# Attention's outputs as fp16 pairs, turned to features inside attention, and an out-projection on them

## What is computed

```python
def trunk_layer(x, xt, ...):
    h = modulate(rms_norm(x, g_attn), sh_a, sc_a)          # and ht for the context tokens
    ... = split_mixer_inputs(h @ w_in, qk_g)               # q, k, v of three head groups
    o = jnp.concatenate([window_attention(...),            # group A, 6 heads
                         neighbourhood_attention(...),     # group B, 4 heads
                         global_block_attention(...)], -1) # group C, 6 heads
    x = x + ga_a * (o @ w_out)
    x = x + ga_f * swiglu(modulate(rms_norm(x, g_ffn), sh_f, sc_f), w_gate, w_up, w_down)
    if update_ctx:                                         # layer 0 only
        ...                                                # the same for xt
```

## Time and profile before

| | before |
|---|---|
| median of 3 runs | 1800.26 us |
| profiled execution, whole | 1800.2 us |
| its span, first to last instruction | 1798.4 us |
| mean granted clock of PE, share of full speed | 0.982 |
| PE busy | 1684.0 us (94%) |
| PE weight loads busy | 1241.0 us (69%) |
| DVE busy | 970.4 us (54%) |
| ACT busy | 662.0 us (37%) |
| POOL busy | 787.5 us (44%) |

### The profile page before, as it was taken

One profiled execution on the slowest core, in us unless ns is written; L12 is line 12 of the kernel. 1 busy time (PEld: TensorE's weight loads), 2 busy tenths in 40 slices (PEclk: granted clock), 3 DMA queues, 4 the chain that ended last, 5 costly groups with the idle time before them and its releaser, 6 DMA issues. The chain is left out here.

```text
span 1798.4 us, 27888 instructions
## 1 busy us (share of the span) xinstructions
PE 1684.0 (94%) x11035; PEld 1241.0 (69%) x11035; DVE 970.4 (54%) x1715; ACT 662.0 (37%) x1218; POOL 787.5 (44%) x575
## 2 busy tenths in 40 slices
PE   7999988977989999999999999997987999999998
PEld 3688877866856678666876687786876645745646
DVE  3544488895458841686428844456995612122112
ACT  3222267775233410233013113225875354053130
POOL 2244435662424563344413343542233657458363
PEclk9999999999989999999999999999999999999999
DMA  9344353322124423245226422443103324334332
GB/s 316 47 107 114 98 139 86 91 59 71 47 71 141 120 82 103 83 131 162 72 70 188 137 62 57 114 101 107 19 2 82 83 71 117 94 90 109 83 82 82
DMA packets 314351, 174.99 MB, mean 97 GB/s; under 512 B 87518, under 2 KB 309614, under 8 KB 314222
## 3 DMA queue, kind: packets, MB, share of 16 engines
q1 hardware_dynamic: 284686, 143.70, 30.3%
q10 hardware_dynamic: 29536, 29.51, 5.1%
HBM read 159.04 MB, written 2.83 MB: 90 GB/s over the span
## 5 line engine op out<-in xcount | busy, mean ns | idle before, releaser
L889 PE MATMUL acc<-act,pair_w 128*128 128x512 f16 x3168 | 582.9, 345 | 7.2 <-ACT act L1283 4.2
L889 PEld LDWEIGHTS acc<-act,pair_w 128*128 128x128 f16 x3168 | 308.8, 99 | 268.2 <-DVE act L1607 10.0
L889 PE MATMUL acc<-act,split_w 128*128 128x512 f32 (+1 forms) x1920 | 381.0, 357 | 8.8 <-DVE act L1871 2.8
L889 PEld LDWEIGHTS acc<-act,split_w 128*128 128x128 f32 x1920 | 308.9, 191 | 62.2 <-DVE act L1871 4.5
L889 PE MATMUL acc<-hidden,split_w 128*128 128x512 f32 (+1 forms) x1584 | 309.2, 357 | 6.6 <-POOL split_w L655 3.6
L652 POOL TENSOR_SCALAR split_w<-raw_w 128x1024 fp32r<-128x1024 f32 (+1 forms) x120 | 126.6, 1055 | 427.6 <-PE acc L889 333.5
L889 PEld LDWEIGHTS acc<-hidden,split_w 128*128 128x128 f32 x1584 | 260.0, 188 | 53.0 <-POOL split_w L655 5.3
L655 POOL TENSOR_TENSOR split_w<-raw_w,split_w 128x1024 fp32r<-128x1024 f32 (+1 forms) x120 | 280.3, 2336 | 10.0
L758 POOL TENSOR_SCALAR pair_raw<-pair_raw,weight_scale 128x1024 f32<-128x1024 f32 x88 | 106.2, 1207 | 357.5 <-ACT pair_w L1457 357.5
L1934 DVE SCALAR_TENSOR_TENSOR mod_acc<-mod_chunk,silu_c,mod_acc 128x256 f32<-128x256 f32 x280 | 223.7, 842 | 4.0
L1632 DVE SCALAR_TENSOR_TENSOR x_t<-acc,mod,x_t 128x512 f32<-128x512 f32 x96 | 60.4, 659 | 257.1 <-PE acc L889 256.6
(11 more groups left out here) (189 smaller groups left out, 1883.3 us busy)
## 6 DMA issues: line engine op xcount, KB each, us to landing
mod_chunk<-in_w_mod ACTq DMA_DIRECT2D x28, 1024.0 KB, 5.2
pair_raw<-in_w_gate SPq DMA_DIRECT2D x44, 512.0 KB, 4.1
pair_raw<-in_w_up SPq DMA_DIRECT2D x44, 512.0 KB, 5.5
raw_w<-in_w_in SPq DMA_DIRECT2D x64, 256.0 KB, 3.7
raw_w<-in_w_down SPq DMA_DIRECT2D x32, 512.0 KB, 4.2
raw_w<-in_w_mod SPq DMA_DIRECT2D x24, 512.0 KB, 4.2
mod_start<-in_w_mod SPq DMA_DIRECT2D x8, 1024.0 KB, 11.7
ks<-q_split SPq DMA_DIRECT2D x64, 96.0 KB, 2.2
```

Of the source, the lines that this page charges most:

```text
L889: mm = pe.matmul(acc[slot][:, a:b], weights[:, part == 2, k, :], moving[:, part == 1, k, a:b], start=(k == 0 and part == 0), stop=(k == n ...
```

## The change

Attention's output is no longer kept as fp32. POOL makes a high and a low fp16 part of each group's output in three passes (`output_high`, `output_whole`, `output_low`) into `o16`. PE turns both parts with fp16 transposes, one feature tile at a time, for latent tokens (part 0) and context tokens (part 1) apart, at steps of attention that the table `OUT_TURNS` fixes; the turned tile goes into one of the three rotating PSUM banks, and one ACT instruction (two for tiles 3 and 4) copies both parts, relatively scaled, into `out16`. Only the turns whose step is past the loop's work come after it.

The out-projection takes fp16 pairs on both sides. Its 8 weight tiles have raw buffers of their own for all 8 (`out_raw`) and four for the pairs (`out_w`). Squares and roundings of tiles 0 to 2 are put into attention's steps on ACT (`OUT_SQUARE_STEP`, `OUT_ROUND_STEP`), one sum and scale into `OUT_SUM_STEP`; those of tiles 3 to 7 stand between ACT's other work during the out-projection. Tiles 3 to 7 are loaded when attention's last output is ready. `residual` takes a gate that has the scales multiplied in. Five small DVE instructions and one small product per layer make the outputs' common scale in the in-projection. The sums of weights, for gate and up also, are one bf16 product of the upper halves of fp32 sums instead of an fp32 one.

```diff
+OUT_ORDER = (0, 1, 2, 5, 6, 7, 3, 4)
+OUT_SUM_STEP = [92, 56]
+OUT_SQUARE_STEP = [(88, 89, 90), (51, 52, 53)]
+OUT_ROUND_STEP = [(94, 95, 96), (58, 59, 61)]
+N_OUT_EARLY = 3
...
+OUT_TURNS = [
+    [(38, 0, 0), (40, 1, 0), (42, 2, 0), (47, 0, 1), (49, 1, 1), (51, 2, 1), (74, 5, 0), (75, 6, 0), (76, 7, 0),
+     (79, 5, 1), (83, 6, 1), (86, 7, 1), (90, 3, 1), (94, 4, 1), (99, 3, 0), (100, 4, 0)],
+    [(26, 0, 0), (29, 1, 0), (37, 2, 0), (50, 5, 0), (53, 6, 0), (60, 7, 0), (66, 3, 0), (68, 4, 0)],
+]
...
+            out += [("o", n) for n, _, _ in turns_at(l, i)]
+            if i == OUT_SUM_STEP[l]:
+                out.append(("w", l))
...
+        out_w = [place(f"out_w{i}", [P, 2, 8, P], F16, split_at_ + (0, 8192, 4096, 12288)[i]) for i in range(4)]
...
-        o = place("o", [P, 6, D], F32)
+        o16 = place("o16", [P, 6, 2, D], F16)
+        out16 = [place(f"out16_{m}", [P, 2, TOK], F16, b0 + where) for m, where in
+                 enumerate((47104, 50176, 53248, 16384, 19456, 56320, 59392, 62464))]
+        out_raw = [raw_w[0], raw_w[1], place("out_raw2", [P, 8, P], F32, b0 + 22528)] + [
+            place(f"out_raw{j}", [P, 8, P], F32, a0 + 4096 * (j - 3)) for j in range(3, KT)]
...
-                    sp.wait_ge(split_ready, ring_of[u] - 1)
+                    if j < 2:
+                        sp.wait_ge(split_ready, ring_of[u] - 1)
+                    elif j < N_OUT_EARLY:
+                        sp.wait_ge(scores, LAYER_STEPS[l][-16] + 1)
+                    else:
+                        sp.wait_ge(o_ready, sum(N_GROUPS[:l + 1]))
...
-                        sp.wait_ge(ot_ps, l * KT + 1)
+                        sp.wait_ge(o_ready, sum(N_GROUPS[:l + 1]))
...
-                    if j in (2, 3):
-                        load_pair(j - 2)
+                    if j in (4, 6):
+                        load_pair(j // 2 - 2)
...
+            def split_out(l, j):
+
+                u = u_out(l) + j
+                pool.wait_ge(out_hi, KT * l + j + 1)
+                pool.tensor_scalar(out_raw[j][:, :, :], out_raw[j][:, :, :], out_scale[:, 1, j:j + 1], 0.0, ALU.mult, ALU.add
+                                   ).then_inc(hi_w, 1)
+                pool.wait_ge(hi_w, ring_of[u] + 1)
+                pool.tensor_tensor(out_w[j % 4][:, 1, :, :], out_raw[j][:, :, :], out_w[j % 4][:, 0, :, :], ALU.subtract
+                                   ).then_inc(split_ready, 1)
...
+                    pool.tensor_tensor(output_piece(k, 0), output_sum(k), inverse_sums(k), ALU.mult).then_inc(o_hi, 1)
+
+                def output_whole(k):
+                    gk = k + sum(N_GROUPS[:l])
+                    pool.wait_ge(o_hi, gk + 1)
+                    pool.tensor_tensor(output_sum(k), output_sum(k), inverse_sums(k), ALU.mult).then_inc(o_mul, 1)
+
+                def output_low(k):
+                    gk = k + sum(N_GROUPS[:l])
+                    pool.wait_ge(o_mul, gk + 1)
+                    pool.tensor_tensor(output_piece(k, 1), output_sum(k), output_piece(k, 0), ALU.subtract).then_inc(o_ready, 1)
...
+                    if k == N_GROUPS[0] - 2:
+                        split_out(l, 0)
+                    output_high(k)
+                    output_whole(k)
+                    output_low(k)
                     if 16 <= k < 20:
                         for i in range(4):
                             bias_tables(k - 16, i)
-                for i in range(4 * N_GROUPS[l] + 8 if l else 0):
+                for i in range(4 * N_GROUPS[l] + 10 if l else 0):
                     if i < 4 * N_GROUPS[l]:
                         minus_top(LAYER_STEPS[l][0] + i)
                     if i == 4 * N_GROUPS[l]:
-                        split_next(0)
+                        split_out(l, 0)
                     if i >= 11 and i % 4 == 3:
-                        take_output((i - 11) // 4)
+                        output_high((i - 11) // 4)
+                    if i >= 12 and i % 4 == 0:
+                        output_whole((i - 12) // 4)
+                    if i >= 13 and i % 4 == 1:
+                        output_low((i - 13) // 4)
...
+                high = weight_sum[:, 2 * f:2 * f + 2].bitcast(BF16)[:, 1:4:2]
+                pe.matmul(mod_ps[:, 0:2], ones16[:, :], high, start=True, stop=True).then_inc(weight_ps, 1)
...
+                def turn_output(n, m, part):
+
+                    free_bank(("o", n))
+                    pe.wait_ge(o_ready, sum(N_GROUPS[:l]) + OUT_GROUPS[l][m, part] + 1)
+                    if n == 0:
+                        pe.wait_ge(masks_ready, 1)
+                    bank = turned_at[BANK_AT["o", n] % 3].bitcast(F16)
+                    for p in range(2):
+                        for t in ((0, 1, 2, 3), (4, 5))[part]:
+                            a = 512 * p + P * (t - 4 * part)
+                            mm = pe.transpose(bank[:, a:a + P], o16[:, t, p, P * m:P * m + P], ident_h[:, :])
+                    mm.then_inc(ot_ps, 1)
...
-                outputs_to_features(0)
...
+                for n, m, part in turns_at(l, g1 + 4 - g0):
+                    turn_output(n, m, part)
...
-                    dense(u % 2, split_w[u % 2], 8, act, width(l), output_tile if j == 0 else last_output if j == KT - 1 else None)
+                    for i, k in enumerate(OUT_ORDER):
+                        if j == 0:
+                            pe.wait_ge(ot_taken, last_turn[k])
+                        if 1 <= j < KT - 2 and i == 1:
+                            sum_out(j + 2)
+                        if j == KT - 1 and i == KT - 1:
+                            sum_first_squares(2 * l + 1, width(l))
+                        for part in (0, 2, 1):
+                            for a, b in parts_of(width(l)):
+                                mm = pe.matmul(acc[u % 2][:, a:b], out_w[j % 4][:, part == 2, k, :], out16[k][:, part == 1, a:b],
+                                               start=(i == 0 and part == 0), stop=(i == KT - 1 and part == 1))
+                    mm.then_inc(unit_done, 1)
...
+                    sc.activation(out_squares[:, :], out_raw[j][:, :, :].rearrange("p k n -> p (k n)"), ACT.Square,
+                                  accum_out=out_sum[:, j:j + 1]).then_inc(out_sq, 1)
...
+                    sc.wait_ge(out_scaled, out_call(l, j))
+                    sc.wait_ge(unit_done, u_out(l) + (j - 3 if j >= 4 else 0))
+                    sc.activation(out_w[j % 4][:, 0, :, :], out_raw[j][:, :, :], ACT.Copy, scale=out_scale[:, 1, j:j + 1]
+                                  ).then_inc(out_hi, 1)
...
+                    if m in (3, 4) and part == 0:
+                        for p in range(2):
+                            i = sc.activation(out16[m][:, p, 0:LAT].rearrange("p (r c) -> p c r", r=ROWS),
+                                              bank[:, 512 * p:512 * p + LAT].rearrange("p (c r) -> p c r", r=ROWS), ACT.Copy, scale=scale)
+                    else:
+                        a, b = ((0, LAT), (LAT, TOK))[part]
+                        i = sc.activation(out16[m][:, :, a:b], bank.rearrange("p (s c) -> p s c", s=2)[:, :, 0:b - a], ACT.Copy, scale=scale)
+                    i.then_inc(ot_taken, 1)
...
+                    if k == 0:
+                        square_out(3)
+                    elif k + 2 < KT:
+                        round_out(k + 2)
+                    if k + 4 < KT:
+                        square_out(k + 4)
...
+                    ve.tensor_scalar(out_gate[:, j, 0:nb], mod[:, l, 2 * KT + j, 0:nb], out_scale[:, 0, j:j + 1], o_back[:, 0:1],
+                                     ALU.mult, ALU.mult).then_inc(out_gated, 1)
+                    ve.wait_ge(out_gated, KT * l + j + 1)
+                    if 1 <= j < KT - 2:
+                        scale_out(j + 2, j + 3, small[:, j + 2:j + 3])
                     ve.wait_ge(unit_done, u_out(l) + j + 1)
-                    residual(j % 2, x_t[:, j, :], l, mod[:, l, 2 * KT + j, :], w)
+                    residual(j % 2, x_t[:, j, :], l, out_gate[:, j, :], w)
```

201 lines of the change are left out of this document (128 added, 73 removed).

## The result

The changed kernel takes 1816.11 us (median of 7 runs, 1808.96 to 1819.86) against 1800.26 us for the kernel before (7 runs, 1796.07 to 1805.84): a ratio of 1.0081, 95% interval 1.0058 to 1.0104. It is slower, by 10 to 19 us. The forecast was 1803, slower by 2.9, with a range up to 1813. The profiled execution took 1816.1 us with a span of 1814.3; the one of before took 1800.2 with 1798.4, so the traces differ by 15.9 us.

A forecast was written before the change was run, and what follows sets the result against it. Attention was taken as held by VectorE with ScalarE close behind, the turn into the out-projection by a chain of small steps. -14.6 + 9 + 0.7 + 10 - 3 + 0.8 = +2.9 on 1800.2 gave 1803 us, range 1788 to 1813.

The forecast's parts named there:

- Layer 0's attention and turn: Layer 0: inserted work costs attention 9 us; the stretch from last weighing through out-projection takes 69.7 against 84.3, gaining 14.6.
- Layer 1's attention: Layer 1's attention: turns, squares, roundings and scale steps inserted between exponential and rounding delay VectorE, costing 10 us.
- The ring of layer 1: Layer 1's out-projection: dependent ScalarE and VectorE laps of 7 to 8 us make TensorE wait 8; stretch 0.7 us longer.
- The sums of weights ... save 3 (bounds 0 and 6): Between dense units: one bf16 product instead of two fp32 ones halves 0.14 us for 44 sums, saving 3 us.
- Norm and down stages of layer 1: Behind layer 1's out-projection: -1.0 us, from shares of the 3 us sums saving and the 0.8 us small costs.
- rival 2: Layer 1's out-projection: TensorE falls to the low clock, units 3 to 7 take 10.36 us each, about 1817; chance 0.12.
- Rival 3: Layer 1's out-projection: loads come later than reckoned and adds block, a stall of 15 us, about 1810; chance 0.11.

The follow-up runs named there:

- experiment 1: Changed kernel with VectorE's last 8 modulation accumulations moved behind the first residual in down stages 1 and 2: 1805.14 us, ratio 1.0025.
- experiment 2: Changed kernel with loads, squares, sums and roundings of weight pairs 0 and 1 moved behind the out-projection's own tiles, both layers: 1809.21 us, ratio 1.0046.
- experiment 9: Changed kernel with GpSimd's split passes of the second next pair behind down tiles 3 and 5 instead of 1 and 2: 1801.71 us, ratio 1.0002.
- experiment 12: Changed kernel with both VectorE's last accumulations and GpSimd's split passes moved later in the down stages: 1800.73 us, ratio 1.0004.
- experiment 3: Kernel before with only the sums of weight squares as one bf16 product instead of two fp32 ones: 1801.51 us, ratio 0.9997.
- the fair pair: Changed kernel and kernel before with bf16 sums, both with later accumulations and later split passes: 1800.73 and 1785.38 us.

## Why the prediction was wrong

The two profiled executions differ by 15.9 us, and the sum had 2.9. Of the 13 between them, 4.6 lie in layer 0's second down stage, 3.1 behind layer 1's norm, 2.0 in layer 1's turn, and 1.6 each in layer 0's turn and layer 1's attention.

- **Layer 0's attention and turn**: right. +9.4 for 9, and 70.1 us for 69.7. The last output was ready 3.1 us after the last weighing (3.0 forecast). To the norm the gain is 13.1 instead of 14.6, mostly because the last weighing itself now starts 5.3 us behind the last exponential (4.1 before).
- **Layer 1's attention**: +11.6 for 10. The steps with inserted work account for 9.1, and for 9.0 to 9.4 in each of the four other kernels (experiments 1, 2, 9, 12) that insert the same. The other 2.5 came at steps 3, 9 and 10, where VectorE waits 1.86 us for a DMA of norm rows (0.74 before) and ScalarE 1.43 us for a DMA of keys. Over the first 14 steps those four differ from before by -0.2, +1.1, +0.8 and +2.3, and the versions of the kernel before by 0.1 to 1.1, so most of this looks like scatter of those landings; no run tested it. The size of an insertion was mis-stated: the three squares cost 0, 0.6 and 0.8 us instead of 0.5, 1.13 and 1.13, a rounding about 0.5 instead of 1.1, and turns cost more than I gave them (the three early ones 2.5 with their neighbours; 1.5 forecast). The errors of the parts offset each other.
- **The ring of layer 1**: the mechanism right (the pairs on ScalarE's lap; experiment 2), 7.1 us of waits for 8. Its times came out within half a microsecond: after the last output, roundings 4 to 7 end at 24.9, 32.1, 38.6 and 44.5 us (24.8, 32.5, 38.8 and 44.4 forecast). The place of the waits didn't: TensorE stood mostly at the sum of pair 0's squares, ahead of unit 3, which the prediction left out of TensorE's list, and less at weight tiles 3 to 7. The stretch costs +2.6 instead of +0.6, 0.75 of it because the last output is ready 9.95 us behind the last exponential (1372.48 to 1382.43) instead of 9.2.
- **"The sums of weights ... save 3 (bounds 0 and 6)": this is the step that failed.** Each saves 0.11 us, 4.8 in all, more than forecast. But the sum took it as kept. In the kernel before, this edit alone brings no gain that can be told (experiment 3), because down stage 2 grows by 4.9 us. In the changed kernel the same stage grows by 4.8, with the same 5.35 us wait; without that wait the changed kernel takes 1805.1 (experiment 1), within the range. The prediction never read the down stages; it assumed, without saying so, that what TensorE gains ahead of a stage reaches the end. The 2.87 us wait there was in the trace of before, and VectorE's 9.9 us for eight accumulations too. No run takes the sums out of the changed kernel alone; that they are the trigger there too rests on the 0.66 us above, which all versions with bf16 sums share.
- **Norm and down stages of layer 1**: +2.1 for -1.0. The last DMA lands 1.5 us later in this execution than before. The first two down stages grow from 46.3 to 46.9 us each, half of it waits for GpSimd's splits and half slower units, which takes back what the sums save there.
- **What was low besides**: without the sums the prediction had +5.9 for the change. In the traces of the fair pair (experiment 12) it is +10.8: 3.3 of the difference lie in the two turns, 1.2 in the two attentions, 0.4 in the rest.
- **Rivals**: rival 2 (layer 1's clock) would have given 1817, almost the measured time, but did not occur: one unit ran at a reduced clock (0.84 in 1401 to 1412), at a cost of 1.7 us, and the waits behind it were 0.2 to 0.8 us each. The right number would have come from a wrong reason. Rival 3's stall of 15 us was 7.1.

VectorE's waiting for GpSimd is the mechanism behind the failed step. When VectorE's first accumulation starts 0.15 us ahead of GpSimd's pass it takes 0.35 us; when they start 0.02 us apart it takes 1.22 us and ends 0.14 us behind GpSimd's. The Trainium skill (SBUF — State Buffer, "SBUF: two separate sides") calls this an exclusive lock taken for a whole instruction by whichever starts first. The traces agree about the whole instruction: each accumulation beside a pass takes about as long as the pass, and the 4.0, 6.5, 6.9, 9.9 and 12.3 us that eight equal accumulations took go with none, two, two, five and six passes beside them (experiment 9 moved passes away). By the starts that the profile gives they don't agree about the order: VectorE is 0.02 us ahead at 855.67 and still takes as long as GpSimd. The prediction used that rule for one instruction of layer 1 and did not ask where else both engines work side by side with TensorE waiting behind.

What stays open: why down products follow each other every 0.174 us in some stages and every 0.177 in others (layer 0's first stage in the fair pair of experiment 12); why the third stage and layer 1's in-projection differ by 2.8 us there, 2.1 of it in the in-projection's products; and why layer 1's down units take 0.04 us more in every version of the changed kernel (33.3 against 33.0 us for the last eight).

## What to carry to other kernels

A gain upstream is only a gain if every later stage is held by the engine that gained: before adding small savings up, look in each later stage for an idle gap of that engine, however short, and for who ends it. A tenth of a microsecond can decide it: 0.13 us settled here which of two engines waits, and the stage behind took 4.8 us more. Where two engines take turns and a third waits behind them, try moving one engine's passes to a place with slack: two lines were worth 14 us here. And compare a change with its side edits taken out and given to the other side as well. These two lines bring the changed kernel level with the one before, which looks as if they had undone its loss; but the kernel before gains from them too, and with the bf16 sums and two moves, without the change, it is the fastest. Against that the change costs 15 us.

## What the runs showed of the hardware

- Eight VectorE accumulations of 128x256 fp32 elements take 4.0 us alone and up to 12.3 us beside GpSimd passes of 1.1 to 2.4 us, three times as long. An accumulation of 0.35 or 0.49 us alone takes 1.2 to 2.6 us beside a pass, about the length of the pass. A start 0.02 or 0.15 us ahead decides whether the first takes 1.22 or 0.35 us.
- After a wait of 5.35 us TensorE's granted clock was 0.60 over the next 3.6 us, then 1.00; in experiment 3, after a wait of the same length, it was 0.61 over 6.8 us. After the 2.87 us wait in the same place of the kernel before, it stayed at 1.00. (1.00 is 2.4 GHz, 0.50 is 1.2.)
- At a granted clock of 1.00 the products of a down stage of layer 0 follow each other every 0.174 us in some executions and every 0.177 in others, 1.3 us over a stage of 384.
- A bf16 product of two columns stands 0.03 us between dense units where two fp32 ones stand 0.14 us.
